# Expert loop: bias products of 128 rows become pairs of 64-row products, and the first sums need one product a bank

## What is computed

```python
def expert_block(args):
    xe, e = args
    gate = jnp.minimum(xe @ w_gate[e] + b_gate[e], SWIGLU_LIMIT)
    up = jnp.clip(xe @ w_up[e] + b_up[e], -SWIGLU_LIMIT, SWIGLU_LIMIT)
    act = (up + 1) * (gate * jax.nn.sigmoid(SWIGLU_ALPHA * gate))
    return act @ w_down[e] + b_down[e]

yb = lax.map(expert_block, (xb, block_e)).reshape(-1, h.shape[-1])
y = yb[dest] * sorted_w[:, None].astype(h.dtype)
return jax.ops.segment_sum(y, sorted_tok, num_segments=t)
```

## Time and profile before

| | |
|---|---|
| median of 3 runs | 2926.16 us (2921.34 to 2933.83) |
| profiled execution | 2921.05 us, span 2919.2 us |
| TensorE busy | 2851.9 us, 98% |
| VectorE busy | 2016.2 us, 69% |
| ScalarE busy | 1607.6 us, 55% |
| GpSimd busy | 552.1 us, 19% |
| HBM | 218 GB/s over the span, 381 to 402 GB/s in the loop |

### The profile page before, as it was taken

How to read it: one execution, slowest core, us unless ns; L and a number is a source line. 1 busy time by engine, 2 the same in 40 slices (tenths; PEclk the granted TensorE clock), 3 DMA queues, 4 the chain that set the end, 5 groups by cost and what they waited for, 6 DMA issues and landing times. The chain is left out here.

```text
span 2919.2 us, 41458 instructions
## 1 busy us (share of the span) xinstructions
PE 2851.9 (98%) x15052; PEld 2298.8 (79%) x15052; DVE 2016.2 (69%) x2238; ACT 1607.6 (55%) x1753; POOL 552.1 (19%) x479
## 2 busy tenths in 40 slices
PE   8999999998999999998999899999999999999999
PEld 4688888765788888876788688888888888888887
DVE  8642234587622336846753799999999999999998
ACT  5342323346522324435632677777777777777775
POOL 1012100113012000013100222223232222222221
PEclk9999999998999999999999999999999999999999
DMA  8422221220122322110022799999999999999995
GB/s 350 168 88 111 101 101 73 91 89 30 65 95 87 130 87 94 58 58 16 1 87 89 298 402 386 386 386 385 386 385 384 388 381 385 386 382 383 381 385 219
DMA packets 88923, 638.87 MB, mean 219 GB/s; under 512 B 10448, under 2 KB 11664, under 8 KB 26096
## 3 DMA queue, kind: packets, MB, share of 16 engines
q1 hardware_dynamic: 78592, 599.97, 52.5%
q0 software_dynamic: 9936, 36.75, 4.7%
q10 hardware_dynamic: 288, 0.65, 0.1%
HBM read 611.28 MB, written 26.05 MB: 218 GB/s over the span
## 5 line engine op out<-in xcount | busy, mean ns | idle before, releaser
L3252 DVE TENSOR_TENSOR arena_rounded<-arena,arena_rounded 128x2048 fp32r<-128x2048 f32 x420 | 950.9, 2285 | 91.3 <-ACT arena_rounded L3248 91.3
L3248 ACT ACTIVATE arena_rounded<-arena 128x2048 fp32r<-128x2048 f32 x420 | 801.4, 1918 | 209.8 <-PE banks L265 133.8
L263 PE MATMUL banks<-arena_rounded,operand_rounded 128*128 128x512 f32 (+1 forms) x2064 | 817.5, 396 | 4.2 <-DVE small_rounded L3544 2.2
L264 PE MATMUL banks<-arena_rounded,operand_rounded 128*128 128x512 f32 (+1 forms) x2064 | 801.6, 388 | 0.0
L265 PE MATMUL banks<-arena_rounded,operand_rounded 128*128 128x512 f32 (+1 forms) x1504 | 583.1, 388 | 0.0
L263 PEld LDWEIGHTS banks<-arena_rounded,operand_rounded 128*128 128x128 f32 x2064 | 387.8, 188 | 85.1 <-DVE arena_rounded L3252 4.5
L264 PEld LDWEIGHTS banks<-arena_rounded,operand_rounded 128*128 128x128 f32 x2064 | 388.1, 188 | 76.6 <-issue 1.0
L265 PEld LDWEIGHTS banks<-arena_rounded,operand_rounded 128*128 128x128 f32 x1504 | 282.4, 188 | 58.8
L264 PE MATMUL banks<-arena_rounded,arena_rounded 128*128 128x512 f32 (+1 forms) x688 | 266.7, 388 | 0.0
L263 PE MATMUL banks<-operand_rounded,arena_rounded 128*128 128x512 f32 (+2 forms) x712 | 265.8, 373 | 0.1
L265 PE MATMUL banks<-operand_rounded,arena_rounded 128*128 128x512 f32 (+2 forms) x712 | 263.5, 370 | 0.0
(11 more groups left out here) (523 smaller groups left out, 3875.7 us busy)
## 6 DMA issues: line engine op xcount, KB each, us to landing
arena<-in_gate SPq DMA_DIRECT2D x140, 1024.0 KB, 7.6
arena<-in_up SPq DMA_DIRECT2D x140, 1024.0 KB, 7.8
arena<-in_down SPq DMA_DIRECT2D x140, 1024.0 KB, 5.7
arena<-in_dense SPq DMA_DIRECT2D x62, 2048.0 KB, 7.6
arena<-in_dense SPq DMA_DIRECT2D x6, 1024.0 KB, 4.8
small<-in_rows SPq DMA_DIRECT2D x7, 512.0 KB, 7.3
resid<-in_x SPq DMA_DIRECT2D x4, 512.0 KB, 8.2
expert_sums<-operand SPq DMA_DIRECT2D x4, 512.0 KB, 4.4
```

The lines of the kernel that those rows point to most:

```text
L263: nc.tensor.matmul(out, left[0], right[0], start=start, stop=False)
L264: nc.tensor.matmul(out, left[0], right[1], start=False, stop=False)
L3248: nc.scalar.activation(high[q % NHI], raw[:, q, :], ACT.Copy).then_inc(high_ready, 1)
L3252: nc.vector.tensor_tensor(low[q], raw[:, q, :], high[q % NHI].bitcast(F32), ALU.subtract).then_inc(low_ready, 1)
```

## The change

The layout of the biases changes: the left column half now holds, in the four groups of rows, gate high, gate low, up high, up low. The right half holds down low, zeros, down high, down high. `spread_t` gets the high part in group 0 too (a copy more on ScalarE, and twice the products at line 2873, to both halves of the bank's rows). Then one product of 128 rows gives a bank of the first sums. `pick` has ones for all four groups. In the loop, the biases of gate and up are added together after pieces 1 and 5, as two products of 64 rows: rows 0 to 63 end the sum in gate's bank, rows 64 to 127 open the sum in up's bank.

```diff
-        sp.dma_start(both[0:NE], e["bias_dram"][0, 0:2].rearrange("r e c -> e r c")).then_inc(e["bias_in"], 16)
-        sp.dma_start(both[NE:2 * NE], e["bias_dram"][1, 0:2].rearrange("r e c -> e r c")).then_inc(e["bias_in"], 16)
-        for row, col, h in ((2, 0, 0), (3, 0, 0), (2, 1, 1)):
-            sp.dma_start(both[row * NE:(row + 1) * NE, col, :], e["bias_dram"][h, 2]).then_inc(e["bias_in"], 16)
+        for row in range(4):
+            sp.dma_start(both[row * NE:(row + 1) * NE, 0, :], e["bias_dram"][row % 2, row // 2]).then_inc(e["bias_in"], 16)
+        for row, h in ((0, 1), (2, 0), (3, 0)):
+            sp.dma_start(both[row * NE:(row + 1) * NE, 1, :], e["bias_dram"][h, 2]).then_inc(e["bias_in"], 16)
@@ scalar of route
         nc.scalar.activation(e["spread_t"][2 * NE:4 * NE, :], k.psum[2 * NE:4 * NE, 3, :], ACT.Copy).then_inc(spread_high, 1)
+        nc.scalar.activation(e["spread_t"][0:NE, :], k.psum[0:NE, 3, :], ACT.Copy).then_inc(spread_high, 1)
@@ tensor of route
-            i = nc.tensor.matmul(k.psum[2 * NE:4 * NE, 3, tokens(t)], e["spread_twice"][:, t, :], k.cst("ident"),
-                                 start=True, stop=True, tile_position=(0, 2 * NE))
+            for half in range(2):
+                i = nc.tensor.matmul(k.psum[2 * NE * half:2 * NE * (half + 1), 3, tokens(t)], e["spread_twice"][:, t, :],
+                                     k.cst("ident"), start=True, stop=True, tile_position=(0, 2 * NE * half))
@@ gpsimd of route
-        nc.gpsimd.memset(e["bias"][3 * NE:, D:2 * D].bitcast(F32), 0.0).then_inc(bias_zero, 1)
+        nc.gpsimd.memset(e["bias"][NE:2 * NE, D:2 * D].bitcast(F32), 0.0).then_inc(bias_zero, 1)
...
-        nc.gpsimd.memset(e["spread_t"][0:2 * NE, :].bitcast(F32), 0.0).then_inc(bias_zero, 1)
+        nc.gpsimd.memset(e["spread_t"][NE:2 * NE, :].bitcast(F32), 0.0).then_inc(bias_zero, 1)
+        pool.wait_ge(bias_zero, 2)
@@ tensor of experts, the first sums
-            pe.wait_ge(e["bias_in"], 16 * 5)
+            pe.wait_ge(e["bias_in"], 16 * 7)
             for t in range(ST):
                 for c in range(2):
-                    for n in range(2):
-                        at = n * D + c * NB
-                        i = nc.tensor.matmul(k.psum[:, first_bank(c, t), :], e["spread_t"][:, t * P:(t + 1) * P], e["bias"][:, at:at + NB],
-                                             start=(n == 0), stop=(n == 1))
-                    i.then_inc(biased, 1)
+                    at = D + c * NB
+                    nc.tensor.matmul(k.psum[:, first_bank(c, t), :], e["spread_t"][:, t * P:(t + 1) * P], e["bias"][:, at:at + NB],
+                                     start=True, stop=True).then_inc(biased, 1)
@@ tensor of experts, open_products
-                    i = exact_product(nc, k.psum[:, r, :], x, (w[0][:, j, :], w[1][:, j, :]), start=(d == 0), stop=False)
-                if q % 2 == 1:
+                    i = exact_product(nc, k.psum[:, r, :], x, (w[0][:, j, :], w[1][:, j, :]), start=(r % 2 == 0 and d == 0),
+                                      stop=(r % 2 == 1 and d == DT - 1))
+                if q % 4 == 1:
                     if q == 1:
                         pe.wait_ge(chosen, b + 1)
-                    at = (r % 2) * D + (r // 2) * NB
-                    i = nc.tensor.matmul(k.psum[:, r, :], e["choice"], e["bias"][:, at:at + NB], start=False, stop=True)
+                    at = (r // 2) * NB
+                    for n in range(2):
+                        rows = slice(2 * NE * n, 2 * NE * (n + 1))
+                        i = nc.tensor.matmul(k.psum[:, r + n, :], e["choice"][rows], e["bias"][rows, at:at + NB],
+                                             start=(n == 1), stop=(n == 0))
@@ shape_constants
-    put("pick", (i[:, None] % NE == np.arange(NE)) & (i[:, None] < 2 * NE))
+    put("pick", i[:, None] % NE == np.arange(NE))
```

## The result

| | before | after |
|---|---|---|
| median | 2924.44 us (22 runs, 2919.59 to 2933.83) | 2932.62 us (22 runs, 2928.18 to 2942.5) |
| profiled execution | 2921.05 us, span 2919.2 us | 2929.82 us, span 2928.0 us |
| one block of the loop | 35.487 us | 35.763 us |
| first product of the loop after the stage's first matmul | 9.88 us | 10.88 us |

The account below looks back on a forecast made before the run. TensorE's gap-free line of matmuls was taken to bound the loop. Loop +12.7, first sums -0.4 and route 0 gave +12.3 us on a median of 2926.2: 2938.5 us, range 2922 to 2947.

Parts of the forecast that it names:

- What bounds the kernel: Expert loop: TensorE's matmuls run without a hole, so whatever is added or taken moves the end by the same amount.
- The first pair: Pair after piece 1: steps of 0.32, about 0.43 and 0.34 us; 0.64 us in place of two products' 0.455.
- The second pair: Pair after piece 5: taken to cost the same as the one after piece 1, +0.18 us a block.
- 70 x 0.181: Loop: two pairs in each of 35 blocks, each 0.181 us dearer than two full products, +12.7 us.
- What the removed products cost: Loop: the four 128-row bias products removed from each block cost only their steps, 4 x 0.227 = 0.91 us.
- VectorE has 2.7 us a block to spare: Loop: VectorE's slack covers the shifted signals, cost nothing; without that cover at most 0.4 us a block.
- rival B: Loop: the change of mode costs nothing; -16.1 us, 2910.1 us (-0.55%); chance 0.07.
- The first sums: Before the loop: sixteen products become eight, the transposes start 0.4 us earlier; -0.4 us, between -0.9 and 0.
- The route: Bias loading and spreading before the loop: seven DMAs of 32 rows, extra products and copy; 0, from -0.5 to +1 us.
- A: Loop: a pair's two products don't run side by side; +29 us less 0.4, 2954.8 us (+1.0%); chance 0.07.
- C: Loop: the gaps stay but the weights are loaded in them; -3.6 us, 2922.6 us, no change; chance 0.06.

Follow-up runs that it names:

- no_bias: The kernel before without any gate or up bias products in the loop; 2903.79 us, a block 34.653 us.
- full_rows: The changed kernel with both bias products of each pair taking all 128 rows; 2928.51 us, ratio 1.0014 to the kernel before.
- split: The changed kernel with the two 64-row products of each pair taken apart, each alone between 128-row matmuls; 2980.37 us.
- pair_twice: The changed kernel with each pair of 64-row bias products issued twice in a row; 2948.64 us.
- once: The changed kernel with both pairs of a block after piece 1, one behind the other; 2924.86 us, ratio 0.9998 to the kernel before.
- full_first: The changed kernel with 128-row bias products, paired only after piece 1; the second half's two come after pieces 5 and 7 as before; 2920.3 us.
- five_dmas: The changed kernel with the left half of the biases loaded by two DMAs of 64 rows instead of four of 32; 2943.51 us.

## Why the prediction was right, and where it was not

**What bounds the kernel.** Right for what is added to TensorE's line: 35 x 0.277 = +9.7 us from the loop and -0.9 us from the start make the +8.8 us of the spans. Not right for what is taken away, of which the forecast said the same: no_bias took 0.983 us out of the line and the block got shorter by 0.834, because VectorE is closer than the forecast had it, see below.

**The first pair: right.** 0.318, 0.428 and 0.338 us were forecast as 0.32, 0.43 and 0.34, from the lone pair of the earlier trace rows. That the row was of another type (plain fp32) and of another stage made no difference; what mattered was the same neighbours. The sum by steps is 0.318 + 0.003 + 0.428 + 0.338 - 4 x 0.227 = 0.18 us over two full products, forecast 0.181. Full_rows shows that the cost is the 64 rows', split that it is per visit, pair_twice that a pair in 64-row mode costs one step. "Changing tiling mode (not just tile) drains the TensorE" (the Trainium skill, TensorEngine Tiling (Array Packing), Key Properties): the trace agrees, with 0.09 us at the change to 64 rows, and as much at the change back if the open load there is the 0.11 us of the next step; it adds that open load at both.

**The second pair: mis-sized.** The term is "70 x 0.181": it took both pairs to have the same neighbours. The second is followed by line 3356's transposes, whose weight load exposes 0.057 us and not 0.11: 0.054 us a block too much, 1.9 us in all. The rows of before show these transposes behind piece 5, so it could have been read.

**What the removed products cost: mis-sized.** "4 x 0.227 = 0.91 us" leaves out the wake. A product in the stream takes 0.253 us with it. Pairs make a wake too, so of the four removed only two wakes go, those in pieces 4 and 8: 0.05 us a block, 1.8 us. Its cause is open; no run varied it by itself.

**VectorE: the step was wrong in kind, small in size here.** "VectorE has 2.7 us a block to spare, so I cost this at nothing." The 2.7 us are an average over the block. In the 15.4 us ahead of a block's end VectorE has no hole to speak of, and its last operation was 0.37 us ahead of need, not 2.7. The change takes 0.25 us of cover out at piece 7 and the second pair's longer way gives most of it back, so the lead falls to 0.27 us only and no gap opens. The rest of the block is 0.016 us longer all the same, 0.6 us in all, in several steps of 2 to 5 ns behind the block's start; that this is VectorE's is not shown. The forecast also had the signal of a pair's piece come 0.41 us later. The pair that raises it starts 0.32 us behind the last weight product, 0.09 later than the lone product did, and its record is 0.11 us longer (0.50 for 0.39): 0.2 us. With pairs at no price that give-back is missing, and the loss would be nearer to the 0.15 us of no_bias and once, a third of rival B's 0.45 us a block. No run had such pairs, so this is an estimate from those two.

**The first sums: the right sign, by luck.** Forecast -0.4, measured -0.9 us (start and first block, with the seven DMAs in it). The sign to look for, a loop that starts 0.4 us sooner after the first of the sums, did not come: it started 1.2 us later. The forecast had the gather land at 1657.9, 5.4 us after its issue; it took 6.8 us. The gain came from a place that the forecast didn't look at: the first block's stall on the DMA of the sums. That the DMA lands before ScalarE needs it is what the rows show; that the eight sums alone do this isn't shown, since start and first block vary together over all kernels.

**The route: wrong in its parts.** "7 x 0.48 = 3.4 us" priced each issue by the three of the earlier trace rows. But the first two bias DMAs take 1.2 us of SyncE each, of 256 KB before and of 128 KB after, and the others 0.45: 4.8 us instead of 3.9. The bias tile wasn't late for it (TensorE waits 0.71 us for it, before 0.94), but the issues behind it were, and with them the gather. Forecast 0, from -0.5 to +1; the +1.0 us of the loop's start is at its upper end. That the gather would land later was in no term of the forecast.

**The rivals.** A fell: 3 ns between the two of a pair. B fell: the gaps are there. C fell: the steps behind the gaps are 0.34 us. Forecast +12.3, measured +8.2 by the medians and +8.8 by the spans; of the 3.5 us between forecast and spans, 1.9 are the second pair, 1.8 the wakes, 0.5 the start, and -0.6 the rest of the block. The changed median, 2932.6 us, lies in the range of 2922 to 2947, and the mechanism of its main term is shown. The two errors of the loop point the same way; those of the start, a loop that begins 1.0 us later and a first block that is 1.6 us shorter, cancel in part.

## What to carry to other kernels

Count a change of the array's mode per visit, from a row with the same neighbours on both sides: packing two small products into one step pays only in a stream of such products, or where one visit takes all of them. A slack given as a share of busy time says nothing about the stretch that a step is moved out of: before moving work of the bounding engine, find the longest run of gap-free work on the next engine, and by how much its last operation is ahead. Sum steps from start to start, with the five or so behind the one that is changed; the busy share and the view of waits showed none of this loss.

## What the hardware showed that I had not expected

- A half product alone costs as much as a pair: 0.66 us over none, against 0.253 us for a full product (split, after, no_bias).
- A full bias product slows the five steps behind it by 0.026 us together; two side by side cost 0.466 us, two apart 0.506 (full_first, before). Behind the eight transposes of before the steps are long in the same way (0.224, 0.231, 0.236, then 0.233 and 0.231).
- TensorE lost 0.06 to 0.09 us at a block's start where VectorE ended 0.15 to 0.17 us ahead (once, no_bias, full_rows, split), with no wait in the profile; with 0.27 us of lead it lost 0.005 us or less, with 0.37 us nothing.
- Two DMAs with an outer dimension of 2 ran at 52 GB/s and were waited for 15.3 us, where the queues together had moved 387 GB/s and more shortly before (five_dmas).
- The first two of the bias DMAs took 1.2 us of SyncE each, for 128 KB as for 256 KB, and the next 0.45. It is not the start of the row that does it: the issues ahead of them, of line 2777, go 0.50, 0.43, 0.79 and 1.19 us (after). What does is open.
